# FFN 2 of a two-block transformer layer: six of eight weight pairs by seven products, x added to in the output, squares on ScalarE

## What is computed

```python
h2 = rms_norm(x, g_ff[l])
x = x + jnp.square(jax.nn.relu(h2 @ w_ff1[l])) @ w_ff2[l]
```

## Time and profile before

| | us |
|---|---|
| time, median of 3 runs | 2574.9 (2574.84 to 2575.89) |
| span of the profiled execution | 2573.7 |
| PE busy | 2567.3 |
| DVE busy | 2015.8 |
| ACT busy | 1451.4 |
| POOL busy | 536.5 |
| HBM read / written | 503.75 MB / 2.10 MB |

### The profile page before, as it was taken

One profiled execution on the slowest core, in us unless ns is written; L12 is line 12 of the kernel. 1 busy time (PEld: TensorE's weight loads), 2 busy tenths in 40 slices (PEclk: granted clock), 3 DMA queues, 4 the chain that ended last, 5 costly groups with the idle time before them and its releaser, 6 DMA issues.

```text
span 2573.7 us, 34186 instructions
## 1 busy us (share of the span) xinstructions
PE 2567.3 (100%) x11501; PEld 2134.4 (83%) x11501; DVE 2015.8 (78%) x2102; ACT 1451.4 (56%) x1615; POOL 536.5 (21%) x1034
## 2 busy tenths in 40 slices
PE   9999999999999999999999999999999999999999
PEld 8888888888888888888878888888888888888888
DVE  6767888666988888888886655566679988998895
ACT  5546666445565555555555557774455555555553
POOL 2212221233112112222133120003322112211121
DMA  8666666766688888888787655556666766666674
GB/s 274 210 206 212 216 197 208 255 214 209 209 238 246 245 241 244 247 242 243 240 291 216 210 183 195 174 191 211 223 202 215 231 206 218 201 220 206 206 228 154
DMA packets 291153, 564.76 MB, mean 219 GB/s; under 512 B 28512, under 2 KB 41872, under 8 KB 290544
## 3 DMA queue, kind: packets, MB, share of 16 engines
q1 hardware_dynamic: 247616, 502.25, 59.0%
q0 software_dynamic: 43264, 61.18, 10.5%
q10 hardware_dynamic: 176, 0.07, 0.0%
HBM read 503.75 MB, written 2.10 MB: 197 GB/s over the span
## 4 chain that ended last, share of the span: by engine, by line
PE 97%; DVE 1%; DMA 1%; SPq 0%; DVEq 0%; ACT 0%; issue 0%; ACTq 0%
PE pair L2491 22%; PE pair L2486 22%; PE pair L2495 22%; PE pair L2776 8%; PE aux L2776 6%; PE aux L2761 3%; PE aux L2755 3%; PE aux L2758 3%; PE pair L2758 1%; PE pair L2755 1%; PE pair L2761 1%; PE aux L2653 0%; DMA raw<-in_w_ffn_down 0%; PE aux L2648 0%; PE pair L2573 0%; PE pair L2566 0%
## 5 line engine op out<-in xcount | busy, mean ns | idle before, releaser
L845 ACT ACTIVATE w_hi<-raw 128x1024 fp32r<-128x1024 f32 (+1 forms) x786 | 818.2, 1053 | 722.1 <-PE pair L2495 571.4
L1499 DVE TENSOR_TENSOR w_lo<-raw,w_hi 128x1024 fp32r<-128x1024 f32 (+1 forms) x788 | 937.7, 1214 | 342.1 <-ACT w_hi L845 323.2
L2486 PE MATMUL pair<-w_hi,lhs_hi 128*128 128x512 f32 x1568 | 422.6, 391 | 0.8 <-ACT lhs_hi L897 0.8
L2491 PE MATMUL pair<-w_hi,lhs_lo 128*128 128x512 f32 x1568 | 419.7, 389 | 0.6 <-DVE lhs_lo L1552 0.5
L2495 PE MATMUL pair<-w_lo,lhs_hi 128*128 128x512 f32 x1568 | 419.7, 389 | 0.0
L766 POOL DMA_DIRECT2D arena<-arena x528 | 262.4, 603 | 668.9 <-DVE arena L2003 291.0
L2491 PEld LDWEIGHTS pair<-w_hi,lhs_lo 128*128 128x128 f32 x1568 | 294.2, 188 | 63.0 <-DVE lhs_lo L1552 1.4
L2495 PEld LDWEIGHTS pair<-w_lo,lhs_hi 128*128 128x128 f32 x1568 | 294.0, 188 | 62.2 <-DVE w_lo L1499 1.0
L2486 PEld LDWEIGHTS pair<-w_hi,lhs_hi 128*128 128x128 f32 x1568 | 292.2, 188 | 60.6 <-ACT lhs_hi L897 1.2
L2486 PE MATMUL pair<-w_hi,low_hi 128*128 128x512 f32 (+1 forms) x992 | 263.4, 387 | 0.0
L2491 PE MATMUL pair<-w_hi,low_lo 128*128 128x512 f32 (+1 forms) x992 | 262.0, 386 | 0.0
(11 more groups left out here) (366 smaller groups left out, 3244.1 us busy)
## 6 DMA issues: line engine op xcount, KB each, us to landing
raw<-in_w_ff SPq DMA_DIRECT2D x128, 1024.0 KB, 5.2
raw<-in_w_in SPq DMA_DIRECT2D x118, 1024.0 KB, 5.3
raw<-in_w_ffn_down SPq DMA_DIRECT2D x44, 1024.0 KB, 5.1
raw<-in_w_ffn_gate SPq DMA_DIRECT2D x80, 512.0 KB, 6.6
raw<-in_w_ffn_up SPq DMA_DIRECT2D x80, 512.0 KB, 7.5
raw<-in_w_out SPq DMA_DIRECT2D x32, 1024.0 KB, 5.7
arena<-arena POOLq DMA_DIRECT2D x840, 32.0 KB, 4.4
xres<-sums POOLq DMA_DIRECT2D x36, 512.0 KB, 9.8
```

The lines of the kernel that those rows point to most:

```text
L845: nc.scalar.activation(w_hi[:, at.slot(p, k), :, 0:width], raw[:, at.raw_slot(p, k), 2 * h:2 * h + 2, 0:width], ACT.Copy).then_inc(hi_read ...
L1499: v.tensor_tensor(w_lo[:, at.slot(p, k), :, 0:n], raw[:, at.raw_slot(p, k), 2 * h:2 * h + 2, 0:n], w_hi[:, at.slot(p, k), :, 0:n].bitcast( ...
L2486: nc.tensor.matmul(ps[:, t, 0:n], hi_t[:, ch, tok], w_hi[:, s, c, 0:n], start=start and k == 0 and c == 0, stop=False)
L2491: nc.tensor.matmul(ps[:, t, 0:n], lo_t[:, ch, tok], w_hi[:, s, c, 0:n], start=False, stop=False)
```

## The change

- `FIVE` becomes (1, 3, 4, 6, 7), used in block 0, and `SIX` = (0, 1, 3, 4, 6, 7) is used in blocks 1 to 6. The forms of pairs 0 and 1 are made apart (`pair_forms`), that of pair 1 in `ffn2_first` already.
- The sums have three buffers in FFN 2 (`ring`); one of them lies over `xres` and the constants, which FFN 2 no longer needs there.
- x is stored to the output before block 0, all columns but the last 512. The panels' results of those columns are copied by ScalarE into `gates` and `hid` (`copy_part`), and GpSimd adds them to the output in HBM by accumulating DMAs (`add_part`). The last 512 columns stay in `xres` as before.
- The squares are made by ScalarE (`relu_squares`).
- In `seven`, in FFN 1 too, the product of S2 and T2 comes after that of S4, and after those of S1 and S3 where the unit isn't the last; `recombine` names its halves the other way round. The second turned hidden block is taken inside `recombine`, and the first two groups of p2 wait for one turned block each.
- The orders of ScalarE and VectorE within a turn are written anew, as far ahead as unit 3 of the next turn.

The core of the diff:

```diff
-FIVE = (0, 1, 3, 5, 7)
+FIVE = (1, 3, 4, 6, 7)
+SIX = (0, 1, 3, 4, 6, 7)
...
+    t_lo2 = place("t_lo2", [P, TOK, D], F32R, xres_at)
+    t_hi2 = place("t_hi2", [P, 2, N], F32R, con_at)
...
+    ring = [(over_x(xres), [t_hi2[:], t_lo2[:, :, 2 * N:3 * N]], over_x(t_lo2)),
+            (halves(t_sum[0]), halves(t_hi), halves(t_lo[0])),
+            (halves(t_sum[1]), halves(t_hi1), halves(t_lo[1]))]
...
+            sp.wait_ge(evac_done, At("out2").panel(2) + 1 + EVAC_CREDIT)
+            sp.dma_start(token_rows(out[0])[:, :, 0:3 * N], xres[:, :, 0:3 * N]).then_inc(x_stored, 16)
...
+            def add_part(j, i):
+
+                pool.wait_ge(sums_copied, i * 3 + (COPIES1 + j + 1))
+                pool.sem_inc(moving, 1)
+                pool.dma_start(token_rows(out[0])[:, :, j * N:(j + 1) * N], hid if j == 1 else gates,
+                               accum_op=ALU.add).then_inc(parts_added[j % 2], 16)
...
+            with pool.Fori(0, TURNS2 - 1) as i:
+                for n in range(2):
+                    move(i * 2 + (NB1 + T_FF2 + 1 + n))
+                for j in range(3):
+                    add_part(j, i)
```

ScalarE:

```diff
+            def relu_squares(rows):
 
                 for t in range(TOK):
-                    nc.scalar.activation(dst[:, t, :], src[t], ACT.Relu, scale=x_inv[:, t:t + 1])
+                    nc.scalar.activation(rows[:, t, :], rows[:, t, :], ACT.Relu, scale=x_inv[:, t:t + 1])
+                act.drain()
+                nc.scalar.activation(rows, rows, ACT.Square)
                 act.drain().then_inc(act_ready, 1)
...
+            def copy_part(at, p, j, i):
+
+                panel_done(at, p)
+                if p < 4:
+                    act.wait_ge(flipped, i * 2 + (NB1 + T_FF2 + 3 + j))
+                if j == 2 or not isinstance(i, int) or i > 0:
+                    act.wait_ge(parts_added[j % 2], i * 16 if j == 1 else i * 32 + 8 * j)
+                nc.scalar.activation(hid if j == 1 else gates, pairs[at.pair(p)][:], ACT.Copy
+                                     ).then_inc(sums_copied, 1)
...
+                if units == FIVE:
+                    hi_sums(3, n, units)
+                hid_turn(b, 0, T_FF2 - 1)
+                hi_ordinary(at, 2, None)
+                hi_seven(at, 3, None)
+                hi_sums(4, n, units)
...
                     nxt = At("ffn2", i + 1)
-                    for u in range(2):
-                        hi_sums(u, n + 1, True)
-                        hi_seven(nxt, u, None)
+                    hi_sums(0, n + 1, SIX)
+                    copy_part(at, 4, 2, i)
+                    hi_seven(nxt, 0, None)
+                    hi_sums(1, n + 1, SIX)
+                    hi_seven(nxt, 1, None)
+                    hi_sums(3, n + 1, SIX)
```

VectorE:

```diff
             lo(at, 1, 4, 6)
+            pair_forms(2, one_pair, one_sum)
             dve.wait_ge(s_hi_ready, 2)
...
             lo(at, 1, 6, 8)
-            sums_seven(first, 1, TURNS1, False)
+            sums_seven(first, 1, TURNS1, FIVE)
+            dve.wait_ge(s_hi_ready, 3)
+            v.tensor_tensor(one_lo[:], one_sum[:], one_hi[:].bitcast(F32), ALU.subtract)
+            dve.drain().then_inc(s_ready, 1)
...
-                unit_pair(at, 2, n, False, five)
+                if units == FIVE:
+                    sums_seven(at, 3, n, units)
+                    lo_sums(3, n, units)
+                    dve.wait_ge(x_stored, 16)
                 hid_turn(b)
-                unit_pair(at, 4, n, False, five)
-                unit_pair(at, 6, n, False, five)
-                hid_turn(b + 1, 4)
+                lo_ordinary(at, 2)
+                lo_blocks(at, 3)
+                sums_seven(at, 4, n, units)
+                lo_sums(4, n, units)
+                lo_blocks(at, 4)
+                lo_ordinary(at, 5)
+                sums_seven(at, 6, n, units)
+                sums_seven(at, 7, n, units)
+                lo_sums(6, n, units)
+                lo_blocks(at, 6)
+                lo_sums(7, n, units)
+                lo_blocks(at, 7)
                 lo(at, 2, 0, 2)
...
                     nxt = At("ffn2", i + 1)
                     lo(at, 5, 0, 2)
-                    sums_seven(nxt, 0, n + 1, False, True)
+                    sums_seven(nxt, 0, n + 1, SIX)
                     lo(at, 5, 2, 4)
-                    lo_sums(0, n + 1, True)
-                    add_x(at, 4, 2 * N)
-                    sums_seven(nxt, 1, n + 1, False, True)
+                    lo_sums(0, n + 1, SIX)
+                    sums_seven(nxt, 1, n + 1, SIX)
                     lo_blocks(nxt, 0)
+                    lo_sums(1, n + 1, SIX)
+                    sums_seven(nxt, 3, n + 1, SIX)
                     add_x(at, 5, 3 * N)
                     lo_blocks(nxt, 1)
-                    lo_sums(1, n + 1, True)
+                    lo_sums(3, n + 1, SIX)
```

TensorE, in `seven`:

```diff
-                product(q0[:, 0, :], tokens(0, c + 1), block_of(B22), five)
-                pe.wait_ge(t_lo_ready, sevens(i, u, five) * 2 + 2)
-                mm = product(q0[:, 1, :], form(S2), sum_of(T2), True)
-                if last:
-                    mm.then_inc(products, 1)
-                product(aux[:, 3, :], form(S4), block_of(B21), five).then_inc(gran_used, 2)
-                if five and u == 0:
-                    bank_free(at, 1)
-                product(q1[:, 1, :], form(S1), sum_of(T1), True)
-                mm = product(q1[:, 0, :], form(S3), sum_of(T3), True)
+                product(q0[:, 0, :], tokens(0, c + 1), block_of(B22), fresh)
+                product(aux[:, 3, :], form(S4), block_of(B21), fresh).then_inc(gran_used, 2)
+                if last:
+                    second().then_inc(products, 1)
+                if u == 0:
+                    bank_free(at, 1)
+                pe.wait_ge(t_lo_ready, sevens(i, u, units) * 2 + 1)
+                product(q1[:, 0, :], form(S1), sum_of(T1), True)
+                mm = product(q1[:, 1, :], form(S3), sum_of(T3), True)
                 if last:
                     mm.then_inc(products, 1)
-                product(aux[:, 2, :], tokens(1, c + 1), sum_of(T4), five).then_inc(t_used, 1)
+                else:
+                    second()
+                product(aux[:, 2, :], tokens(1, c + 1), sum_of(T4), fresh).then_inc(t_used, 1)
```

More of the change, by code:

```diff
@@ L445, in two_blocks @@
     sums_added = [sem(f"sums_added{j}") for j in range(4)]
+    parts_added = [sem(f"parts_added{j}") for j in range(2)]
+    x_stored = sem("x_stored")
     qk2_sq = sem("qk2_sq")
@@ L691, in _ @@
                 load(At("ffn2_last"), 6 + j, w_ff2_2[0], j * N, TURNS2 * (2 * N))
-            last = At("ffn2_last")
-            for j in range(3):
-                sp.wait_ge(evac_done, last.panel(6 + j) + 1 + EVAC_CREDIT)
-                sp.dma_start(token_rows(out[0])[:, :, j * N:(j + 1) * N],
-                             xres[:, :, j * N:(j + 1) * N]).then_inc(out_done, 16)
             for n, (t, c0, c1) in enumerate(TAIL):
@@ L2413, in block2 @@
                 lo(at, 2, 0, 2)
-                recombine(at, n, 0, five)
+                if units == SIX:
+                    dve.wait_ge(parts_added[0], i * 32)
+                    dve.wait_ge(parts_added[1], i * 16)
+                recombine(at, n, 3, units, lambda: hid_turn(b + 1, 4))
                 lo(at, 2, 2, 4)
                 dve.wait_ge(act_ready, b + 3)
-                for t in range(TOK):
-                    v.scalar_tensor_tensor(act_f[:, t, :], gates[:, 1 - t, :], x_inv[:, t:t + 1],
-                                           act_f[:, t, :], ALU.mult, ALU.mult)
@@ L2430, in block2 @@
-                if not five:
-                    first_forms()
-                lo(at, 4, 0, 4)
-                add_x(at, 3, N)
+                flip(b + (2 + T_FF2), by_chunk(gates), n_split=1)
+                lo(at, 3, 0, 4)
+                if units == FIVE:
+                    pair_forms(0, zero_pair, zero_sum)
+                lo(at, 4, 0, 4)
+                dve.wait_ge(act_ready, b + 4)
                 flip(b + (3 + T_FF2), by_chunk(hid), n_split=1)
@@ L2467, in _ @@
                 lo(at, 7 + j, 0, 4)
-                add_x(at, 6 + j, j * N)
             for n, (t, c0, c1) in enumerate(TAIL):
@@ L2742, in _, with ordinary @@
             gemm(at, 1, wide)
-            def ordinary(at, u, five=False):
+            def ordinary(at, u, units=SEVEN):
                 p, k0 = unit(u)
@@ L2755, in ordinary @@
                         nc.tensor.matmul(bank[t, w], lhs_hi[:, ch, tok], w_hi[:, s, w, :],
-                                         start=c == 0 and (u == 0 or (five and u == 2 and (t, w) == (1, 0))), stop=False)
+                                         start=c == 0 and (u == 0 or (units == SIX and u == 2 and (t, w) == (1, 0))), stop=False)
                     for t, w, tok in parts:
@@ L2761, in ordinary, with seven, product @@
                         mm = nc.tensor.matmul(bank[t, w], lhs_hi[:, ch, tok], w_lo[:, s, w, :], start=False,
```

(20 more changed lines are left out.)

276 lines of the change are left out of this document (155 added, 121 removed).

## The result

The changed kernel takes 2615.05 us (median; 2614.66 to 2617.61) against 2575.16 for the kernel before on the same chip: 1.0157 times as long, interval 1.0142 to 1.0171. The profiled execution has a span of 2613.0 us, 39.3 more than that of before. I forecast 2600.5 us and a range of 2588 to 2615: the direction and the places were right, the size was 14.6 us short, and the time lies 0.05 us above the range.

A forecast was written before the change was run, and what follows sets the result against it. TensorE was taken as the bound. From the profiled 2573.7 us: -4.8 for fewer matmuls, +21.6 for six seam turns, +8.8 for block 0, giving 2599.3, plus 1.2 to the median: 2600.5 us, range 2588 to 2615.

The forecast's parts named there:

- What bounds it: FFN 2: TensorE alone sets the time, busy for all of an 84.00 us turn; VectorE has 8.4 us of slack.
- the sign: Whole kernel: slower, by 1.0%; chance 0.90 of slower by more than 0.2%.
- the places: FFN 2: TensorE pauses before unit 0's tenth matmul at each seam, before unit 6, and four times in block 0.
- -4.8 us for 21 matmuls: FFN 2, blocks 0 to 6: seven units moved, each saving 3 matmuls of 0.228 us, 4.8 us less.
- the third rival: After each seam: 12 matmuls at the lower clock, 0.23 us more each, 16.6 us in all, 2617 us; chance 0.06.
- Seam, 2.9 a turn: Six seams of FFN 2: TensorE waits 2.9 us each for VectorE's panel 5 addition, behind a longer VectorE list.
- Unit 6, 0.7 a turn: Later in a seam turn: TensorE waits for VectorE's low blocks of unit 6, 0.7 us, bounds 0 and 1.5.
- Block 0, 8.8: Block 0 of FFN 2: four stalls of 2.5, 2.5, 1.5 and 2.3 us, together 8.8; bounds 4 and 10.
- `recombine`: FFN 1 and FFN 2: first result ready 0.7 us later, covered by 1.05 us; cost nothing, 3 us at most.
- the store of x: Ahead of block 0's weights: 10.5 us of transfer hidden by four weight buffers; cost 0, bounds 0 and 3.
- the accumulations: FFN 2: GpSimd's accumulating transfers into HBM land after 10 us, bounds 6 and 20, and cost nothing.
- the end: Last panel: its accumulation lands at 2572, before the span's close at 2573.7; cost 0, or +1.7 with a 13.0 landing.

The follow-up runs named there:

- hold5: The kernel before with five unneeded VectorE operations put ahead of panel 5's addition at each of FFN 2's six seams; 2610.49 us (1.0134).
- seam_x: The changed kernel with VectorE's panel 5 addition and unit 1's low blocks moved ahead of unit 3's sums at FFN 2's seams; 2602.99 us (1.0106).
- fifteen: The changed kernel with 15 matmuls, not 9, between panel 5 and the wait for its bank in unit 0; 2603.22 us (1.0106).
- hold3: The kernel before with three unneeded VectorE operations put ahead of panel 5's addition at each of FFN 2's six seams; 2590.94 us (1.0057).
- order2: The changed kernel with the same instructions in a third order on VectorE and ScalarE, found with GpSimd's moves at 13.3 us; 2587.40 us (1.0048).
- no_adds: The changed kernel without FFN 2's 24 accumulating DMAs, leaving out its part of three quarters of the output columns; 2618.73 us (1.0168).

## Why the prediction was wrong in size

- **What bounds it, the sign, the places: right.** A pause before the tenth matmul of unit 0 that VectorE's addition ends, one later in the turn, four in block 0, no idle time in VectorE's list. -4.8 us for 21 matmuls is right.
- **The step that failed is the clock.** The sum put its cost at nothing: I left it to the third rival at 0.06, "as the stall is short", and what was to show the forecast included a granted clock of 1.00. It fell to 0.50 behind each of the six seams, and that cost about 9.8 us. hold5 shows that such a pause does this in the kernel before as well; seam_x, fifteen, hold3 and order2 show that shorter ones in the turns do not. That no row of before showed the low level was a reason for a wide range, not for a small chance: TensorE had no pause there, so the trace could not speak. The section of the Trainium skill that I named, "Why this matters for your kernels" of "TensorE: Matmul & The Clock Gate", says that idle gaps between bursts of matmuls can put the clock back to half. The trace agrees: 0.50 behind each of the six pauses of 3.34 to 3.48 us between starts. The rival's own price, 12 matmuls at 0.23, was too high: some 8 at 0.20, so it put the case at 2617 where adding 9.8 to my sum gives 2610.3.
- **Seam, 2.9 a turn: mis-sized.** 3.25 and 0.1 for the restart. VectorE's list was 13.55 us (2201.75 to 2215.30), I had 13.65. But TensorE wanted the pair 10.47 us after the list began, not 10.79, as the small gaps in front of the seam were gone, and starts 0.17 after the drain. +2.5 over the six.
- **Unit 6, 0.7 a turn: mis-sized.** 0.94 and a restart, +2.1, inside its bounds.
- **Block 0, 8.8: right.** 7.9, with restarts 8.3. Two of its rows name ScalarE, where I had VectorE's low blocks of units 4 and 6. VectorE ends those at 1966.49 and 1978.64, and the matmuls start 0.15 us behind, so the forecast's list holds: ScalarE ended another granule at nearly the same moment.
- **Nothing for `recombine`, the store of x, the accumulations, the end: right** in that no wait names them and no_adds did not make the kernel faster. My 10 us for an accumulation's landing was 7.0.
- **Ahead of FFN 2 the span was 1.2 us longer.** I had no term for it. It isn't the change's: hold3, which is the kernel before up to there, reaches the same matmul 1.4 us later than the profiled run of before.
- The small gaps that before had in FFN 2 (1.4 us) went, and the median lies 2.05 above the span, not 1.2.

2.5 + 9.8 + 2.1 - 0.5 + 1.2 - 1.4 + 0.9 is 14.6, the whole miss. What stays open is which pauses between 2.4 and 2.9 us lower the clock: block 0's first, 2.74 to 2.76 in all ten kernels that have it, did so in seven of the profiled runs and not in three.

## What to carry to other kernels

An engine with slack in the sum can still be late at one place: lay its list against the bound engine's wants at the seam, and price the order, not the total; the same 73.7 us of VectorE gave turns of 89.1, 87.0 and 84.8 us. Where TensorE is the bound and has never paused, a new pause of 3 us has two prices, itself and the clock behind it (half as much again here), and the second belongs in the sum. When work is moved to close a gap, follow what each moved piece releases: two pieces in the wrong places, one too late and one ahead of a wait, cost 35 us through a chain of moves.
